# The delta rule's 64x64 products, laid over the four quarters of the TensorE array

## What is computed

```python
def step(S, inp):
    r_t, w_t, k_t, v_t, kk_t, a_t = inp
    sa = jnp.einsum('bhvk,bhk->bhv', S, -kk_t)
    S = S * w_t[:, :, None, :] + sa[..., None] * (kk_t * a_t)[:, :, None, :] + v_t[..., None] * k_t[:, :, None, :]
    return S, jnp.einsum('bhvk,bhk->bhv', S, r_t)

S, y = lax.scan(step, wkv_prev.astype(f32), seq)
```

## Time and profile before

| | us |
|---|---|
| median of 3 runs | 1610.33 |
| lowest, highest | 1607.25, 1612.68 |
| the profiled execution | 1609.88 |
| its span, from first to last instruction | 1608.1 |
| TensorE (PE) busy in it | 1525.8 |
| VectorE busy | 468.9 |
| mean granted clock of TensorE | 0.976 |

### The profile page before, as it was taken

One profiled execution on the slowest core, in us unless ns is written; L12 is line 12 of the kernel. 1 busy time (PEld: TensorE's weight loads), 2 busy tenths in 40 slices (PEclk: granted clock), 3 DMA queues, 4 the chain that ended last, 5 costly groups with the idle time before them and its releaser, 6 DMA issues.

```text
span 1608.1 us, 39699 instructions
## 1 busy us (share of the span) xinstructions
PE 1525.8 (95%) x18077; PEld 1111.9 (69%) x18077; DVE 468.9 (29%) x1007; ACT 221.0 (14%) x479; POOL 158.4 (10%) x197
## 2 busy tenths in 40 slices
PE   6998989999996999999989999999999999999995
PEld 4766867777774777889654567576776757677672
DVE  2389221111008356263421120212212021221203
ACT  3143210000003411232220000000000000000001
POOL 4137000000000323106100000000000000000000
PEclk9999999999997999998999999999999999999998
DMA  9645044435432410204479999899999989999992
GB/s 292 189 148 137 1 136 128 157 106 179 127 111 62 134 55 2 54 4 122 161 283 414 411 370 403 323 400 363 371 358 366 403 328 399 361 369 360 363 405 92
DMA packets 186098, 379.80 MB, mean 236 GB/s; under 512 B 42255, under 2 KB 125423, under 8 KB 185802
## 3 DMA queue, kind: packets, MB, share of 16 engines
q1 hardware_dynamic: 180352, 365.84, 62.9%
q0 software_dynamic: 2944, 10.49, 1.7%
q10 hardware_dynamic: 2634, 0.92, 0.2%
HBM read 373.23 MB, written 3.98 MB: 235 GB/s over the span
## 4 chain that ended last, share of the span: by engine, by line
PE 89%; DVE 8%; DMA 1%; ACT 1%; issue 1%; SPq 0%; POOL 0%; DVEq 0%; ACTq 0%
PE bk L1575 28%; PE bk L1592 14%; PE bk L1062 11%; PE bk L747 8%; PE bk L1075 5%; PE bk L1559 2%; PE bk L1496 2%; PE bk L1543 2%; PE bk L1155 2%; PE bk L977 2%; DMA ring<-in_w_in_even 1%; PE bk L1089 1%; DVE left L2143 1%; DVE tops L2141 1%; PE bk L1099 1%; DVE kT L2315 1%
## 5 line engine op out<-in xcount | busy, mean ns | idle before, releaser
L1575 PE MATMUL bk<-part,xe 128*32 128x352 f32 x6144 | 468.9, 460 | 2.3 <-DVE xe L2565 2.3
L1575 PEld LDWEIGHTS bk<-part,xe 128*32 128x32 f32 x6144 | 322.4, 110 | 137.1 <-issue 68.0
L1592 PE MATMUL bk<-part,hidT 128*32 128x256 f32 x4224 | 235.2, 379 | 1.1 <-DVE hidT L2592 1.1
L1592 PEld LDWEIGHTS bk<-part,hidT 128*32 128x32 f32 x4224 | 153.7, 109 | 75.9 <-DVE hidT L2592 2.1
L1062 PE MATMUL bk<-xn,ring 128*128 128x288 f32 x704 | 173.6, 410 | 3.7 <-DMA ring<-in_ffn_up 3.7
L2588 DVE TENSOR_TENSOR hp<-sg,bk 128x352 f32<-128x352 f32 x48 | 37.4, 779 | 448.1 <-PE bk L1575 448.1
L1062 PEld LDWEIGHTS bk<-xn,ring 128*128 128x128 f32 x704 | 135.3, 192 | 41.7 <-issue 3.9
L747 PE MATMUL bk<-xg,ring 128*128 128x288 f32 x336 | 89.1, 424 | 10.4 <-DMA ring<-in_w_in_even 8.8
L747 PE MATMUL bk<-mx,ring 128*128 128x288 f32 x384 | 96.2, 409 | 0.0
L747 PEld LDWEIGHTS bk<-xg,ring 128*128 128x128 f32 x336 | 65.6, 198 | 30.2 <-issue 9.5
L747 PEld LDWEIGHTS bk<-mx,ring 128*128 128x128 f32 x384 | 72.0, 190 | 20.4 <-issue 0.9
(11 more groups left out here) (498 smaller groups left out, 1372.9 us busy)
## 6 DMA issues: line engine op xcount, KB each, us to landing
part<-in_moe_gate SPq DMA_DIRECT2D x136, 704.0 KB, 6.8
part<-in_moe_up SPq DMA_DIRECT2D x136, 704.0 KB, 7.1
part<-in_moe_down SPq DMA_DIRECT2D x128, 704.0 KB, 7.2
ring<-in_rwkv_w_rkv SPq DMA_DIRECT2D x24, 512.0 KB, 3.8
ring<-in_ffn_gate SPq DMA_DIRECT2D x22, 512.0 KB, 5.7
ring<-in_ffn_up SPq DMA_DIRECT2D x22, 512.0 KB, 6.8
ring<-in_ffn_down SPq DMA_DIRECT2D x22, 512.0 KB, 4.6
ring<-in_w_in_even SPq DMA_DIRECT2D x16, 512.0 KB, 5.7
```

Of the source, the lines that this page charges most:

```text
L1575: last = mm(banks[g][32 * c:32 * c + 32, 0:FQ], xe[:, k, 32 * g:32 * g + 32], parts[ph % 3][:, FH * k + FQ * c:FH * k + FQ * c + FQ], star ...
L1592: last = mm(down_bk[g // 2][32 * q:32 * q + 32, 256 * (g % 2):256 * (g % 2) + 256], hidT[:, half, g, 32 * m:32 * m + 32], parts[ph % 3][:, ...
```

## The change

All products with both halves alike are laid over the four quarters: for par = 1 the output half (in X·M: the input half) is the other one. The copies that read such a result put it back, in two half copies where one stood; one transposing instruction per group becomes three. The phases go, so each group of a level, W, T and y is complete by itself. In the old states the output half alternates with the sample. The eight bonus instructions move from before the levels to two at the end of levels 1 to 4.

```diff
+    def swapped(copy, dst, src):
+        for a in range(2):
+            last = copy(dst(half_(a)), src(half_(1 - a)))
+        return last
+
+    def of_parity(x, o):
+        return x.rearrange("p h (n o t) -> p (h n) o t", o=2, t=TS)[:, :, o]
...
-        def product(q, p2, ph, lhs, rhs):
+        def product(q, p2, lhs, rhs, swapped):
             for hp in range(KC):
                 for cc in range(2):
-                    par, r = cc ^ ph, half_(cc)
-                    last = mm(bk[GRP[q % 3][par]][r, hp * CH:(hp + 1) * CH], lhs[r, p2, par, hp], rhs[r, p2, par, hp],
-                              start=True, stop=True)
+                    for par in range(2):
+                        r, out = (half_(cc ^ (par & s)) for s in (swapped, 1 - swapped))
+                        last = mm(bk[GRP[q % 3][par]][out, hp * CH:(hp + 1) * CH], lhs[r, p2, par, hp], rhs[r, p2, par, hp],
+                                  start=True, stop=True)
...
+            for p2 in range(2):
+                pe.wait_ge(y_ok, 2 * (j - 1) + p2 + 1)
+                pe.wait_ge(c_ok, 2 * (j - 1) + p2 + 1)
+                product(4 * (j - 1) + p2, p2, Cj[j % 2], Y, 0).then_inc(lv_mm, 1)
             if j < 5:
                 krv_job(40 + 2 * (j - 1))
...
+            for p2 in range(2):
+                pe.wait_ge(m_ok, 2 * (j - 1) + p2 + 1)
+                pe.wait_ge(x_ok, 2 * (j - 1) + p2 + 1)
+                product(4 * (j - 1) + 2 + p2, p2, X, M, 1).then_inc(lv_mm, 1)
...
+                for cc in range(2):
+                    for par in range(2):
+                        r = half_(cc)
+                        last = mm(bk[bank_of[f"W{p2}"][par]][half_(cc ^ par), hp * CH:(hp + 1) * CH], GK[r, p2, par, hp, 0:CH],
                                   Vt[r, p2, par, hp], start=True, stop=True)
+            last.then_inc(d_mm, 1)
...
+                    for cc in range(2):
+                        for par in range(2):
+                            r, hp = half_(cc), 4 * half + i
+                            last = mm(bk[bank_of[name][par]][half_(cc ^ par), P * i:P * i + P], Y[r, p2, par, hp],
+                                      AW[r, p2, par, hp], start=True, stop=True)
+                last.then_inc(d_mm, 1)
...
-                            last = mm(new(bk[6 + par][half_(par), hp * 2 * NS:(hp + 1) * 2 * NS]),
+                            last = mm(new(bk[6 + par][half_(par ^ b % 2), hp * 2 * NS:(hp + 1) * 2 * NS]),
...
+                            r = half_(cc)
                             lhs, rhs = ((BG[r, p2, par, hp, CH:P], TU[r, p2, par, hp, CH:P]),
                                         (GK[r, p2, par, hp, CH:P], Vt[r, p2, par, hp]))[term]
-                            last = mm(bk[bank_of[f"y{p2}"][par]][r, hp * CH:(hp + 1) * CH], lhs, rhs,
+                            last = mm(bk[bank_of[f"y{p2}"][par]][half_(cc ^ par), hp * CH:(hp + 1) * CH], lhs, rhs,
...
-                    last = mm(bk[bank_of[f"y{p2}"][par]][r, hp * CH:(hp + 1) * CH], FT[half_(par), c - 1, hp, CH:P],
+                    last = mm(bk[bank_of[f"y{p2}"][par]][half_(c % 2 ^ par), hp * CH:(hp + 1) * CH], FT[half_(par), c - 1, hp, CH:P],
...
-            for par in range(2):
-                last = nc.scalar.copy(AW[:, p2, par, :, CH:P], banked(bank_of[f"W{p2}"][par]))
-            last.then_inc(d_act, 1)
+            nc.scalar.copy(AW[:, p2, 0, :, CH:P], banked(bank_of[f"W{p2}"][0]))
+            swapped(nc.scalar.copy, lambda r: AW[r, p2, 1, :, CH:P], lambda r: banked(bank_of[f"W{p2}"][1])[r]).then_inc(d_act, 1)
...
-        nc.scalar.copy(W2v[0:HD], banked(6)[0:HD]).then_inc(sm_act, 1)
+        for o in range(2):
+            last = nc.scalar.copy(of_parity(W2v[0:HD], o), of_parity(banked(6)[half_(o)], o))
+        last.then_inc(sm_act, 1)
...
+        def turned_pass(p2):
+            V.transpose(X[:, p2, 0].rearrange("p h t -> p (h t)"), Y[:, p2, 0].rearrange("p h t -> p (h t)"))
+            for a in range(2):
+                last = V.transpose(X[half_(1 - a), p2, 1].rearrange("p h t -> p (h t)"),
+                                   Y[half_(a), p2, 1].rearrange("p h t -> p (h t)"))
+            last.then_inc(x_ok, 1)
...
-        for c in range(KC):
-            v_ = VEC["rwkv_r_k"] + c
-            last = V.scalar_tensor_tensor(kT[:, c], rT[:, c], vecT[:, v_:v_ + 1], kT[:, c], ALU.mult, ALU.mult)
-        last.then_inc(rr_ok, 1)
+        def bonus(cs):
+            for c in cs:
+                v_ = VEC["rwkv_r_k"] + c
+                last = V.scalar_tensor_tensor(kT[:, c], rT[:, c], vecT[:, v_:v_ + 1], kT[:, c], ALU.mult, ALU.mult)
+            return last
...
-                    V.transpose(X[:, p2].rearrange("p a h t -> p (a h t)"),
-                                Y[:, p2].rearrange("p a h t -> p (a h t)")).then_inc(x_ok, 1)
+                    turned_pass(p2)
+                last = bonus((2 * j - 2, 2 * j - 1))
+                if j == 4:
+                    last.then_inc(rr_ok, 1)
...
-                V.tensor_copy(TU[:, p2, 1, 4 * half:4 * half + 4], banked4(bank_of[name][1])).then_inc(d_dve, 1)
+                swapped(V.tensor_copy, lambda r: TU[r, p2, 1, 4 * half:4 * half + 4],
+                        lambda r: banked4(bank_of[name][1])[r]).then_inc(d_dve, 1)
```

More of the change, by code:

```diff
@@ L1257, in _ @@
         turned(pe, "A0")
[L1258 to L1265, removed]
+        for p2 in range(2):
+            turned(pe, f"V{p2}")
+            for hp in range(KC):
+                for cc in range(2):
+                    for par in range(2):
+                        r = half_(cc)
+                        last = mm(bk[bank_of[f"W{p2}"][par]][half_(cc ^ par), hp * CH:(hp + 1) * CH], GK[r, p2, par, hp, 0:CH],
                                   Vt[r, p2, par, hp], start=True, stop=True)
-                if ph == 1:
-                    last.then_inc(d_mm, 1)
+            last.then_inc(d_mm, 1)
         turned_s(pe, "M")
@@ L1302, in _ @@
             turned(pe, f"W{p2}")
[L1303 to L1312, removed]
+            for half in range(2):
+                name = f"T{p2}{half}"
+                for i in range(4):
+                    for cc in range(2):
[4 more added lines that the diff above has]
+                last.then_inc(d_mm, 1)
             old_state(p2)
@@ L1354, in _, with products @@
                 last.then_inc(sm_mm, 1)
[L1356 to L1361, removed]
+        def products(p2):
+            for hp in range(KC):
+                for term in range(2):
+                    for cc in range(2):
+                        for par in range(2):
+                            r = half_(cc)
                             lhs, rhs = ((BG[r, p2, par, hp, CH:P], TU[r, p2, par, hp, CH:P]),
                                         (GK[r, p2, par, hp, CH:P], Vt[r, p2, par, hp]))[term]
-                            last = mm(bk[bank_of[f"y{p2}"][par]][r, hp * CH:(hp + 1) * CH], lhs, rhs,
+                            last = mm(bk[bank_of[f"y{p2}"][par]][half_(cc ^ par), hp * CH:(hp + 1) * CH], lhs, rhs,
                                       start=hp == 0 and term == 0, stop=p2 == 0 and cc == 0 and term == 1,
@@ L1378, in from_state @@
         def from_state(c):
-            p2, r = c // 2, half_(c % 2)
+            p2 = c // 2
             for hp in range(KC):
                 for par in range(2):
-                    last = mm(bk[bank_of[f"y{p2}"][par]][r, hp * CH:(hp + 1) * CH], FT[half_(par), c - 1, hp, CH:P],
+                    last = mm(bk[bank_of[f"y{p2}"][par]][half_(c % 2 ^ par), hp * CH:(hp + 1) * CH], FT[half_(par), c - 1, hp, CH:P],
                               Sp[half_(par), (c - 1) % 2, hp], start=False, stop=True, skip_group_check=True)
@@ L1917, in out_rows @@
         def out_rows(p2):
-            for par in range(2):
-                last = nc.scalar.copy(y_rows[:, p2].rearrange("p (h a v) -> p h a v", h=KC, a=2)[:, :, par],
-                                      banked(bank_of[f"y{p2}"][par]))
-            last.then_inc(d_act, 1)
+            rows_of = y_rows[:, p2].rearrange("p (h a v) -> p h a v", h=KC, a=2)
+            nc.scalar.copy(rows_of[:, :, 0], banked(bank_of[f"y{p2}"][0]))
+            swapped(nc.scalar.copy, lambda r: rows_of[r, :, 1], lambda r: banked(bank_of[f"y{p2}"][1])[r]).then_inc(d_act, 1)
         act.wait_ge(sm_mm, sm_at["U"])
@@ L2414, in _ @@
         dve.wait_ge(sm_mm, sm_at["E"])
-        V.tensor_copy(W2v[HD:P], banked(7)[HD:P]).then_inc(sm_dve, 1)
+        for o in range(2):
+            last = V.tensor_copy(of_parity(W2v[HD:P], o), of_parity(banked(7)[half_(1 - o)], o))
+        last.then_inc(sm_dve, 1)
         dve.wait_ge(sm_mm, sm_at["F"])
```

16 lines of the change are left out of this document (removed).

## The result

| | before | after |
|---|---|---|
| median of 4 runs each on one chip, us | 1611.51 | 1583.82 |
| lowest, highest | 1607.25, 1612.78 | 1582.52, 1586.44 |
| profiled execution: its span, us | 1608.1 | 1580.7 |
| TensorE busy, us | 1525.8 | 1489.7 |
| mean granted clock | 0.976 | 0.978 |

The ratio is 0.9835, with a 95% interval of 0.9811 to 0.9859. The change saves 27.7 us. 39.7 were expected: the saving falls 12 us short. The time lies inside the range of 1562 to 1585, 14 us above the forecast of 1570.

What follows compares the result with a forecast made beforehand. It took TensorE, busy for 95% of the span, as the bound, by its pace and chain of waits. Terms summed to 39.7 us saved, 1609.9 - 39.7 = 1570 us (forecast 60%), range 1562 to 1585.

Steps and rivals of the forecast that it cites:

- (c): Clock falls anyway in or after the old states' products, costing 2 to 5 us: 1572 to 1575; chance 12%.
- (d): Bonus instructions not hidden in levels 1 and 2, blocked by POOL, costing 3 to 7 us: 1573 to 1577; chance 8%.
- mixture of paces: Products run at a mixture of paces, giving 1580 to 1610 us; chance 4%.
- Levels: Inverse levels: level 2's C·Y 6.8 us earlier, half clock gone 1.6, faster products in levels 2 to 4 11.6.
- W and T: Products of W (L1265) and T (L1309) on four quarters: 1.9 and 2.3 us saved, VectorE bounding T.
- (a): One input half at a time may write a PSUM bank; levels, W, T, y gain nothing from quarters: 1594; chance 13%.
- (b): Same bank conflict, served one product at a time, 60 for 30 ns per record: 1651, slower; chance 3%.
- old states: Old-state products (L1351) on four quarters take 3.7 us for 9.61: 5.9 us saved.
- L1342's second half: Products behind the old states, at full clock, cost what the first half does: 1.9 us saved.
- y: Products of y (L1364): two runs of 3.88 us at 1.95 each, 3.9 us saved.
- Level 5: Last inverse level, without projection: each group complete by itself, 3.7 us saved before V1's turn.
- out_rows: One ScalarE copy more, which VectorE's mean waits for: 0.6 us lost.

Runs made afterwards that it cites:

- the probe: Kernel after with 256 unread records of 128 columns added ahead of the first level's products: 1589.3 us, executed once.
- both probes: Kernel after with 256 unread records added ahead of the first level's products, once with 64 columns (1587.5 us), once with 128 (1589.3 us).

## Why the prediction was right and wrong

**Right, and shown**: the bound, the sign, and the gain in the levels. That the time lies in the range is in part luck: the forecast and rivals (c) and (d), 80% together, made 1562 to 1578, and 1583.8 fell into the part kept for a "mixture of paces", with 4%, whose cause is not the one found. **Levels**: groups of 128 in 2.02 us for the 1.95 taken. C·Y of level 2 comes 6.5 us earlier, beyond the 2.25 of chance, for 6.8. The bonus is hidden: eight instructions of 510 to 2607 ns, two per level, none ahead of a Y:

```profile
L2325 DVE SCALAR_TENSOR_TENSOR kT<-rT,vecT,kT x8: 510/634/2607, 615.4 to 652.1; 128x288 f32<-128x288 f32 x8
```

Its median is 634 ns for 1554: of the four pairs, two take 3.28 and 4.60 us beside POOL's masks and the other two, with POOL idle, 0.95 each. **W and T** give 3.1 for 4.2: 1.4 for 1.9 from W's start to T's, 1.7 for 2.3 from T's start to F. VectorE is the bound behind T, as forecast, with two copies of 0.69 per T in the chain above, but the stretch is 7.69 us and not 7.05. At W the products are done in 2 us, but now ScalarE's six copies of 0.58 to 0.59 us (L1878 and L572, 675.39 to 678.96) stand on the chain, where the prediction had the next turns hide the added ones. The run with copies shared out gets back 1.7.

**Rivals (a) and (b), the shared bank**, are refuted by the 2.02 us: four quarters with both input halves writing one bank run at 14.8 ns a record from start to start, as L1145, the old L1136, does with a bank for each. The rule of the Trainium skill ("TensorEngine Tiling (Array Packing)", Gotcha 1), that different row tiles cannot access the same PSUM bank at the same time, does not hold for these products. What the Trainium skill puts in "PSUM — Partial Sum Buffer", PSUM: the matmul accumulator, a limit per bank and 32 partitions, agrees with the run.

**Wrong: one step, used for every run of products.** The prediction took "I take 15.8", a pace read off 128 records between two projections, and multiplied it by any length of run: "256 x 14.5 = 3.7 us" for the old states, "Two runs of 3.88 us at 1.95 each" for y. A pace holds only as long as the instructions do. (The reading itself was also slightly off: 150 records in 4.2 us are 56 ns for two and not 58, which moves the term by 0.1 us.) Term by term: old states 5.9 expected, 2.2 gained (7.49 us for 9.71); L1342's second half 1.9 expected, 0.15 gained, since the clock falls here too; the turn of W2v 0.7 expected, 0.27 gained; y 3.9 expected, nothing gained: in its place stand 2.40 and 0.67 us of pauses. Level 5: from its start at 649.82 to V1's turn 7.75 us for 9.8, a gain of 2.0 where 3.7 were expected; without the 1.62 us of pause it is 6.1, the prediction's own figure.

**Rival (c)** came true beside it: the clock fell in that stretch in all traces. The forecast went without it, since the old states would end before the 4.3 us after which the clock had fallen; it fell 4.8 us into L1350, pauses counted. That it would have met L1341's second half without them too is likely from the kernel with the old states on two quarters, but no run shows it. By itself (c) gave 1572 to 1575. Of the 9.7 us missing from L1341 to the chain of states, the four pauses are 6.05 and L1341's second half and the turn of W2v at half clock 2.2; the rest, 1.4, lies in slower records around the pauses (L1350's 128 in 2.21 us and its last 15, already at half clock, in 0.70; L1364's 128 in 2.35 and 2.28, for 1.95). The bounds of 15.8 and 60 ns covered how fast the array can be and left out how fast it is fed. A hint was in the trace of before: in L1351 and L1342, q8 has a transfer every 3.4 to 4.8 us, as this view of 726 to 746 us (slices of 0.5 us) has it, while 128 records take 3.9:

```profile
GB/s 0 0 33 0 0 0 0 0 0 33 0 0 0 0 0 0 0 0 33 0 0 0 0 11 162 250 343 344 317 304 302 323 271 291 299 302 290 282 93 22
```

By itself that shows only that use and supply go together, since the clock is low in part of it. What should have raised the question is the length of the stretch without a long product, some 800 records.

**out_rows** takes 1.78 us on the chain for 1.08, a loss of 0.7 for the 0.6 forecast. From the chain of states to the end of the span 1.8 us are lost in all; the remaining 1.1 lie within what two executions differ by, and no run looks into them.

## What to carry to other kernels

When products get short, ask not only how fast the array can take them but how fast their instructions come: count the records of the longest stretch in which nothing long stands between them, and set its length against 27 to 30 ns per record as a first estimate (the gap of 6 us between two transfers shows that it can be worse). Idle time of TensorE marked as issue in the middle of one line is where to look for that limit; check it against the transfers of the instruction queue. Where a step is bound by it, splitting it over more quarters gained nothing (y) or little (the old states). Larger instructions kept the pauses away in the probe, and so did a long product in between in the levels; that either would make this stretch faster was not tried. And an elementwise step queued ahead of a needed one costs more once the products beside it are faster: 2.78 us of idle time with two quarters, 6.00 with four.

## What the runs showed of the hardware

- TensorE's instructions came in 16 KB transfers, each good for some 126 to 128 records with their weight loads. While it starved they started 3.3 to 4.0 us apart in most cases, about 27 to 30 ns per record, but 5.6 to 7.0 us apart at one place in each of eleven traces.
- All 54 pauses of over 0.35 us ended 1.2 to 1.7 us after such a transfer had landed. They were 0.4 to 3.0 us long. Where TensorE came to a run of short products from longer ones or from a wait, 208 and 232 records ran at 15 ns before the first pause (two kernels); in level 5 it was 154.
- 128 columns in four quarters took 28 ns per record and hardly starved; 64 columns took 14.8 and did.
- A pause was 0.81 us with 3 GB/s of DMA traffic beside it and 1.2 to 1.8 us in the eleven other traces, 189 GB/s in the one of after (one execution against eleven); the instruction transfer ahead of it took 1.18 us there and 0.97 in after.
- The clock fell in the same stretch with pauses and without, for 6.8 or 10.2 us: 6.8 in after, 10.2 in before, in both probes and with the old states alone on two quarters, 6.8 again with y on two as well.
- Both input halves wrote one PSUM bank, on different partition halves, at 14.8 ns per record, the same as with a bank for each.
